# Narrow retention root with VectorE's product from PSUM, and value projections of retention and fox in blocks of 512 columns

## The reference, cut to what matters

```python
q, k, v = h @ w_in[:, rq], h @ w_in[:, rk], h @ w_in[:, rv]      # q and k are rotated, k scaled
o   = causal sum over m of (q_n . k_m) * decay[n, m] * v_m        # the reference does it in chunks of 128
ret = o * rsqrt(mean(o * o, axis=-1) + 1e-6)                      # root mean square of each head
ret_out = silu(h @ w_in[:, rg]) * ret
mix = sigmoid(gate_a) * (nsa_out @ w_proj_a) + sigmoid(gate_b) * (ret_out @ w_proj_b)
```

## Time and profile before

| | |
|---|---|
| median of 3 runs | 2039.71 us (2038.48 to 2040.23) |
| the profiled execution | 2039.96 us |
| its span in the profile | 2037.8 us |
| TensorE busy | 1985.7 us, 97% of the span |
| VectorE, ScalarE, GpSimd busy | 941.1, 730.8, 796.4 us |
| mean granted TensorE clock | 0.99 |

### The profile page before, as it was taken

One profiled execution on the slowest core, in us unless ns is written; L12 is line 12 of the kernel. 1 busy time (PEld: TensorE's weight loads), 2 busy tenths in 40 slices (PEclk: granted clock), 3 DMA queues, 4 the chain that ended last, 5 costly groups with the idle time before them and its releaser, 6 DMA issues.

```text
span 2037.8 us, 25916 instructions
## 1 busy us (share of the span) xinstructions
PE 1985.7 (97%) x9460; PEld 1575.4 (77%) x9460; DVE 941.1 (46%) x1502; ACT 730.8 (36%) x1211; POOL 796.4 (39%) x333
## 2 busy tenths in 40 slices
PE   7999899999999999999999999999999999999998
PEld 6778565688888888888888888776657888888887
DVE  6762655333642464467661105677993341201211
ACT  5233456433431242333313324435544342321321
POOL 4364321144454345435544443231122524444442
PEclk9999999999999999999999999999999999999999
DMA  6355021134757477548633342232122423343341
GB/s 179 83 125 134 21 61 34 36 94 113 185 132 200 119 191 198 142 123 205 174 94 84 102 105 67 67 72 53 32 52 52 104 73 93 93 108 89 93 109 56
DMA packets 156614, 211.16 MB, mean 104 GB/s; under 512 B 15432, under 2 KB 133736, under 8 KB 156392
## 3 DMA queue, kind: packets, MB, share of 16 engines
q1 hardware_dynamic: 142280, 167.34, 33.0%
q10 hardware_dynamic: 14240, 42.54, 7.0%
HBM read 206.69 MB, written 2.10 MB: 102 GB/s over the span
## 4 chain that ended last, share of the span: by engine, by line
PE 48%; issue 31%; POOL 13%; DVE 6%; ACT 1%; DMA 1%; POOLq 0%; ACTq 0%; SPq 0%; DVEq 0%
PE ps L626 15%; PE ps L628 15%; PE ps L627 15%; POOL wlo L590 12%; DVE top L2208 1%; DVE score L2210 1%; DVE ps L2099 1%; PE ps L1044 1%; PE ps L669 1%; PE ps L1067 0%; DMA xrow<-in_x 0%; PE ps L793 0%; PE ps L1087 0%; PE ps L674 0%; DVE score L2193 0%
## 5 line engine op out<-in xcount | busy, mean ns | idle before, releaser
L590 POOL TENSOR_TENSOR wlo<-raw,whi 128x1024 fp32r<-128x1024 f32 (+1 forms) x317 | 781.1, 2479 | 1182.5 <-ACT whi L1336 1160.3
L626 PE MATMUL ps<-hhi,whi 128*128 128x512 f32 x1488 | 590.6, 397 | 5.5 <-DVE hlo L1848 3.3
L628 PE MATMUL ps<-hhi,wlo 128*128 128x512 f32 x1488 | 581.2, 391 | 0.0
L627 PE MATMUL ps<-hlo,whi 128*128 128x512 f32 x1488 | 581.1, 391 | 0.0
L1336 ACT ACTIVATE whi<-raw 128x1024 fp32r<-128x1024 f32 x309 | 316.3, 1054 | 367.9 <-PE ps L628 357.0
L626 PEld LDWEIGHTS ps<-hhi,whi 128*128 128x128 f32 x1488 | 280.7, 189 | 69.8 <-issue 9.3
L628 PEld LDWEIGHTS ps<-hhi,wlo 128*128 128x128 f32 x1488 | 280.4, 188 | 59.4
L627 PEld LDWEIGHTS ps<-hlo,whi 128*128 128x128 f32 x1488 | 280.9, 189 | 57.6 <-issue 1.4
L626 PE MATMUL ps<-hidhi,whi 128*128 (+1 forms) x608 | 236.6, 389 | 0.0
L628 PE MATMUL ps<-hidhi,wlo 128*128 (+1 forms) x608 | 236.5, 389 | 0.0
L627 PE MATMUL ps<-hidlo,whi 128*128 (+1 forms) x608 | 236.5, 389 | 0.0
(11 more groups left out here) (377 smaller groups left out, 2428.6 us busy)
## 6 DMA issues: line engine op xcount, KB each, us to landing
raw<-in_ffn_w SPq DMA_DIRECT2D x264, 256.0 KB, 3.8
raw<-in_w_in SPq DMA_DIRECT2D x154, 256.0 KB, 3.9
trig<-in_ada_w ACTq DMA_DIRECT2D x72, 512.0 KB, 4.5
raw<-in_w_up SPq DMA_DIRECT2D x64, 256.0 KB, 3.9
raw<-in_w_down SPq DMA_DIRECT2D x64, 256.0 KB, 3.9
raw<-in_w_out SPq DMA_DIRECT2D x32, 256.0 KB, 3.9
xrow<-in_x ACTq DMA_DIRECT2D x4, 512.0 KB, 6.8
raw<-in_cmp_k_w SPq DMA_DIRECT2D x8, 256.0 KB, 3.7
```

The source lines that it names most:

```text
L590: last = pool.tensor_tensor(lo, src, hi.bitcast(F32), ALU.subtract)
L626: pe.matmul(out_, lhi, rhi, start=first, stop=False)
L627: pe.matmul(out_, lhi, rlo, start=False, stop=False)
L628: return pe.matmul(out_, llo, rhi, start=False, stop=last)
```

## The change

The mean square of a head becomes a narrow product (four products with one moving column each, into a 128x4 corner of bank 5), so that root and reciprocal work on 128x4; `root_spread` then spreads the reciprocal by four products with the identity into the head's own bank, and VectorE, not GpSimd, multiplies the head by it from PSUM. The steps stand in other places: the roots of heads 0 to 2 and the products of heads 0 and 1 lie in the loop of tiles, head 3 in the attention's round 0, and ScalarE's high parts come one round earlier and more (head 0 ahead of the attention). Both value projections become one block "W" of 512 moving columns with four slabs of 256 rows; the turns of the block before come in its middle.

```diff
-    rvg += [("A", W1["rv"] + 256 * b, 128, ("rv", 256 * b)) for b in range(2)]
+    rvg += [("W", W1["rv"], "rv")]
...
-    dsa += [("A", W2["fv"] + 256 * b, 128, ("fv", 256 * b)) for b in range(2)]
+    dsa += [("W", W2["fv"], "fv")]
...
+                    elif b[0] == "W":
+                        for q in range(4):
+                            load_next(s, w[2 * q * P:2 * (q + 1) * P, b[1]:b[1] + 512].rearrange("(k p) n -> p k n", p=P))
                             s += 1
...
                 for h in range(4):
-                    r, o = SQ[h], rkT[:, h, :]
-                    pool.wait_ge(rt_rcp, h + 1)
-                    pool.tensor_tensor(o, o, r, ALU.mult).then_inc(rt_m, 1)
+                    o = rkT[:, h, :]
                     pool.wait_ge(rt_m, h + 1)
                     pool.wait_ge(pj_silu, h + 1)
                     pool.tensor_tensor(o, o, srg[:, h, :], ALU.mult).then_inc(rt_o, 1)
...
+                        elif b[0] == "W":
+                            banks = []
+                            for q in range(4):
+                                pe.wait_ge(w_split, s + 1)
+                                hi, lo = slab(s, 2)
+                                for t in range(NT):
+                                    if q == 0:
+                                        banks.append(bank(g + t))
+                                    tt = slice(t * P, t * P + P)
+                                    for k in range(2):
+                                        kk = 2 * q + k
+                                        mm = three(ps[:, banks[t], :], hhi[:, kk, tt], hlo[:, kk, tt], hi[:, k, :], lo[:, k, :],
+                                                   kk == 0, kk == 7)
+                                    if q == 3 and t < NT - 1:
+                                        mm.then_inc(pj_mm, 1)
+                                mm.then_inc(w_used, 1)
+                                s += 1
+                                if q == 1:
+                                    post_products(n)
+                            g += NT
+                            continue
...
             def head_sum(h):
                 pe.wait_ge(rt_ev, h + 1)
-                pe.matmul(ps[:, 3 + h % 2, :], cst[:, C_HD128:C_HD128 + P], SQ[h], start=True, stop=True).then_inc(rt_sum, 1)
+                for t in range(NT):
+                    mm = pe.matmul(ps[:, 5, NT * h + t:NT * h + t + 1], SQ[h][:, t * P:t * P + P],
+                                   cst[:, C_HD128:C_HD128 + 1], start=True, stop=True)
+                mm.then_inc(rt_sum, 1)
+
+            def root_spread(h):
+                pe.wait_ge(rt_rcp, h + 1)
+                for t in range(NT):
+                    mm = pe.matmul(ps[:, 3 + h % 2, t * P:t * P + P], root[:, h, t:t + 1].broadcast_to([P, P]), ident,
+                                   start=True, stop=True)
+                mm.then_inc(rt_spread, 1)
...
                     if j == 0 and h >= 2:
-                        pe.wait_ge(rt_root, h - 1)
+                        pe.wait_ge(rt_m, h - 1)
...
                     if x % NT == 2 and 6 <= x:
                         head_sum(x // NT - 1)
+                    if x % NT == 0 and 8 <= x:
+                        root_spread(x // NT - 2)
...
                     if r < n:
                         score_pair(r, 0)
+                        if r == 0:
+                            head_sum(3)
...
                         if part == 1 and r < n:
+                            score_pair(r, 1)
                             if r == 0:
-                                head_sum(3)
-                            score_pair(r, 1)
+                                root_spread(3)
...
+                        if b[0] == "W":
+                            for q in range(2):
+                                high(s + q + SLOTS)
+                            for t in range(NT):
+                                sc.wait_ge(*OUT_DONE[g])
+                                sc.activation(BUF[b[2]][:, t, :], ps[:, g % 4, :], ACT.Copy).then_inc(pj_ev, 1)
+                                g += 1
+                            s += 2
...
                     sc.wait_ge(rt_pv, 4 * h + 4)
+                    sc.activation(SQ[h], ps[:, 3 + h % 2, :], ACT.Square).then_inc(rt_ev, 1)
                     sc.activation(rkT[:, h, :], ps[:, 3 + h % 2, :], ACT.Copy)
-                    sc.activation(SQ[h], ps[:, 3 + h % 2, :], ACT.Square).then_inc(rt_ev, 1)
                     sc.wait_ge(rt_sum, h + 1)
-                    sc.activation(SQ[h], ps[:, 3 + h % 2, :], ACT.Sqrt, bias=col(C_EPS)).then_inc(rt_root, 1)
+                    sc.activation(root[:, h, :], ps[:, 5, NT * h:NT * h + NT], ACT.Sqrt, bias=col(C_EPS)).then_inc(rt_root, 1)
+                retention_high(0)
...
                     if t >= 4:
                         sc.wait_ge(at_pv["nsa"], t - 3)
-                    else:
-                        sc.wait_ge(rt_m, t + 1)
...
-                    for h in {1: (0,), 2: (1,), 3: (2, 3)}.get(r, ()):
+                    for h in {0: (1,), 1: (2,), 2: (3,)}.get(r, ()):
                         retention_high(h)
...
                         x += 1
-                retention_root(0)
+                        if x >= 7 and x % NT == 3:
+                            retention_root(x // NT - 1)
+                        if x >= 9 and x % NT == 1:
+                            retention_scale(x // NT - 2)
+                retention_scale(2)
...
-                ve.reciprocal(SQ[h], SQ[h]).then_inc(rt_rcp, 1)
+                ve.reciprocal(root[:, h, :], root[:, h, :]).then_inc(rt_rcp, 1)
+
+            def retention_scale(h):
+                ve.wait_ge(rt_spread, h + 1)
+                ve.tensor_tensor(rkT[:, h, :], rkT[:, h, :], ps[:, 3 + h % 2, :], ALU.mult).then_inc(rt_m, 1)
...
                         maxima(r, 0)
+                        if r == 0:
+                            retention_root(3)
...
                         maxima(r, 1)
-                        if r < 3:
-                            retention_root(r + 1)
+                        if r == 0:
+                            retention_scale(3)
                         branch_b(r)
```

More of the change, by code:

```diff
@@ L269, in mix_kernel @@
                                                                              "pj_dve", "pj_silu"))
-        rt_qk, rt_sd, rt_pv, rt_ev, rt_sum, rt_root, rt_rcp, rt_m, rt_o, rt_hi, rt_done = (
-            sem(n) for n in ("rt_qk", "rt_sd", "rt_pv", "rt_ev", "rt_sum", "rt_root", "rt_rcp", "rt_m", "rt_o", "rt_hi", "rt_done"))
+        rt_qk, rt_sd, rt_pv, rt_ev, rt_sum, rt_root, rt_rcp, rt_spread, rt_m, rt_o, rt_hi, rt_done = (
+            sem(n) for n in ("rt_qk", "rt_sd", "rt_pv", "rt_ev", "rt_sum", "rt_root", "rt_rcp", "rt_spread", "rt_m", "rt_o", "rt_hi", "rt_done"))
         cm_shift, cm_blk, cm_sig, cm_hid, cm_turn, cm_hidT, cm_out, cm_done = (
@@ L288, in mix_kernel @@
         g = p = r = sl = 0
-        n_out = {"A": 4, "G": 2, "B": 2, "K": 6}
+        n_out = {"A": 4, "G": 2, "B": 2, "K": 6, "W": 4}
         for name, blocks in BL.items():
@@ L327, in mix_kernel @@
             for b in blocks:
-                s += {"A": 2, "B": 2, "K": 1, "G": 0}[b[0]]
+                s += {"A": 2, "B": 2, "K": 1, "G": 0, "W": 4}[b[0]]
                 for x in range(n_out[b[0]]):
-                    if b[0] != "G" and x == {"A": 3, "B": 1, "K": 3}[b[0]]:
+                    if b[0] != "G" and x == {"A": 3, "B": 1, "K": 3, "W": 3}[b[0]]:
                         OUT_DONE[g] = (w_used, s)
@@ L706, in bank, with post_products @@
                     return x % 4
+                def post_products(n):
+                    nonlocal p
+                    for kind, v in turns[n]:
+                        c = chunks[v]
+                        if p >= 4:
+                            pe.wait_ge(pj_dve, p - 3)
+                        if kind == "ms":
+                            pe.wait_ge(pj_ev, out_of[v] + 1)
+                            m = post_ms(name, v)
+                            pe.matmul(ps[:, 4 + p % 4, :], cst[:, C_HD64:C_HD64 + P], SQ[m % 4], start=True, stop=True)\
+                              .then_inc(pj_post, 1)
+                        else:
+                            if c[0] == "rope":
+                                pe.wait_ge(pj_ev, out_of[v] + 1)
+                            else:
+                                pe.wait_ge(pj_dve, post_event[name, "ms", v] + 1)
+                            if name == "nsa" and p == P0["nsa"]:
+                                pe.wait_ge(ld_rest, 16)
+                            perm = c[4] if c[0] == "rope" else c[5]
+                            pe.matmul(ps[:, 4 + p % 4, :], cst[:, perm:perm + P], st[:, v % 4, :], start=True, stop=True)\
+                              .then_inc(pj_post, 1)
+                        p += 1
                 for n in range(len(blocks) + 2):
@@ L785, in projection @@
                                 g += 1
[L786 to L794, removed]
```

(19 more changed lines are left out.)

2 lines of the change are left out of this document (1 added, 1 removed).

## The result

The changed kernel has a median of 2024.12 us over 4 runs (2023.23 to 2024.93), beside 2039.97 us (2038.48 to 2042.08, 4 runs) for the kernel before on the same chip. The ratio is 0.9923, with a 95% interval of 0.9911 to 0.9935: 13 to 18 us faster. The profiled execution took 2024.89 us with a span of 2022.7 us. The forecast was 2024.5.

What follows compares the result with a forecast made beforehand. TensorE, busy 1985.7 of 2037.8 us, was taken as the bound. Terms -3.8 - 3.7 + 2.0 - 9.7 = -15.2 us against the profiled 2039.96 gave 2024.8, forecast as 2024.5, range 2020.5 to 2031.

Steps and rivals of the forecast that it cites:

- Block W for `rv`: At the `rv` projection, 96 wide products in 21.8 us replace two blocks and pauses of 25.5: gain 3.8 us.
- rival B: Skill's price for wide products holds, 0.2 us instead of 1.3 a site: 2.1 us less gain, 2026.6; chance 0.04.
- Block W for `fv`: At the `fv` projection, the block with rotations in its middle ends at 1379.8 for 1383.46: gain 3.7 us.
- the second needs VectorE's norm, done at 1365.2, wait 0 to 0.4: Inside the `fv` block, the second rotation product waits at most 0.4 us for VectorE's 0.75 us norm step.
- W for `fv` from 1346 or so on: Sign expected in the timeline after: the `fv` block starts near 1346, all behind being 12 us earlier.
- The loop: Retention's loop: narrow sums and spreads replace three wide sums on a full TensorE, costing +2.0 us.
- rival C: Coupling in retention's loop: VectorE's product late for heads 2 and 3, sums wait for squares; +3 us, 2027.5; chance 0.12.
- Rounds 0 to 4: Attention's first rounds: without wide reciprocals and GpSimd products, round 5 at 25.6 us instead of 35.75; -9.7 us taken.
- rival A: Attention's start keeps its pauses through the ScalarE-GpSimd chain and stretched normalisations: gain only 9 us, 2030.7; chance 0.13.
- Rival D: Granted clock falls in retention's loop, whose 22.5 us are then worth as much again: slower, 2047; chance 0.03.
- Rival E: Nothing moves in the end, because something late (a load, a slab) sets the pace behind; chance 0.03.
- The range's lower end: 2020.5 us, from retention +1.5, rounds -11, slow stretch behind `fv` shorter by 1.5, and rounding 1.

Runs made afterwards that it cites:

- e1: Kernel before with only the two W blocks, all of retention as before: 2030.87 us, ratio 0.9961.
- e2: Changed kernel with both value projections back in two A blocks, so the retention part alone: 2029.92 us, ratio 0.9949.
- e5: Changed kernel, but ScalarE makes the next slabs' high parts in dsa only after the W block's second slab: 2024.19 us, ratio 0.9913.
- e3: Changed kernel with sums, roots and reciprocals wide again (128x512, no spread) in the new places, VectorE multiplying from SBUF: 2032.15 us, ratio 0.9958.
- e4: Changed kernel with ScalarE's four high parts of retention back in rounds 1, 2, 3 and 3: 2027.3 us, ratio 0.9936.
- e7: Kernel before with eight added products of 512 columns ahead of retention's loop, a pure shift: 2040.04 us, ratio 0.9999.
- e10: The version of e6 run again beside the changed kernel on the same chip: 2022.32 us, ratio to before 0.9912.
- e6: Changed kernel with the held-back slabs of e5 and ScalarE's first high part of retention ahead of its wait for head 3's sum: 2022.48 us, ratio 0.9911.
- e8: Changed kernel with the spreads of heads 0, 1 and 2 done twice: 2026.15 us, ratio 0.9934.

## Why the prediction was right, point by point

**The total** was right, 2024.5 for 2024.12, but not every term, and two errors nearly cancel.

**Block W for `rv`**: 21.76 us, no bank waits, gain 3.8 as forecast. The price of columns was the row's: two blocks of 11.58 less one of 21.76 is 1.4 us, with the same 21.76 in e1 and the same 11.58 in e2. By the Trainium skill, "TensorE: Matmul & The Clock Gate", section "Wait — 56ns, not 53.3ns?", the estimate was 0.2 us a site (rival B). For these forms the traces disagree: 226.7 ns with 512 moving columns and 120.6 with 256.

**Block W for `fv`**: the term that was mis-sized. The step "the second needs VectorE's norm, done at 1365.2, wait 0 to 0.4" took the norm step's length, 0.75 us, from a row in which GpSimd was idle. The norm step ahead of it in the same trace, beside GpSimd's low parts, would have warned:

```profile
1360.03 1.14 DVE L1942 SCALAR_TENSOR_TENSOR st<-st,vec,PT 128x512 f32<-128x512 f32 x1
```

```profile
1358.22 5.21 POOL L590 TENSOR_TENSOR wlo<-raw,whi 128x1024 fp32r<-128x1024 f32 x2 [9.16 <-ACT whi L1336]
```

The change itself lets ScalarE, and behind it GpSimd, start on the next slabs half a block earlier, beside just that step: 1.85 us, a wait of 0.89, and the gain 2.6 instead of 3.7. I had cited such a stretch for the attention and not asked it of `fv`, though the diff moves the two high parts. e5 removes it. The sign "W for `fv` from 1346 or so on" was a slip: 1353.8 less the 11.5 us of the other terms is 1342.3, and W started within 1.5 us of that (1340.75).

**The loop**: +2.3 for +2.0. Sums and spreads did cost 0.81 us for eight records, but the product behind each starts 0.09 us later than behind a wide sum (208.02 to 208.33 for what were 0.22 us). No wait of TensorE in 22.5 us, also for heads 2 and 3: rival C has nothing. The margin is as thin as I had called it: VectorE's product with head 0 ends at 212.05 and head 2's first value product starts at 212.46, 0.4 us later, where I had counted 0.3.

**Rounds 0 to 4**: -9.3 for -9.7, and by the mechanism named: three long reciprocals out of the rounds and the fourth short (e3), high parts one round apart (e4). How the 9.3 divide between the reciprocals and GpSimd's four products is open. Round 0 went as worked out: sum of head 3 after a wait of 0.35, first exponential and second score pair at 4.38 us behind the first (forecast 4.2), round 1 at 7.2 (6.8), round 2 at 11.2 (10.6), round 5 at 26.4 (25.6). The normalisations beside GpSimd never held TensorE over 0.33 us, so rival A did not come; e4 is that rival made true, by placing two high parts in one round, and it cost 2.8 us in the rounds and 3 in time.

**Rival D** (clock in the loop): granted clock 1.00 in both stretches. **Rival E**: the gain arrived whole at the end.

**What I did not see**: that untouched stretches differ by 2 us and more between two executions. I subtracted from one profiled execution, which from round 5 to the second norm is slower than all eleven other traces, also than that of its own program shifted (e7). The terms -3.7 and -9.7 were too large by 1.5 together, the loop's too small by 0.3, and those 1.9 us filled the hole. That the total came within 0.4 us was luck; the parts alone would have given 2026.3, still in the range. The range's lower end was 0.3 us too high by its own sum: 0.5 + 1.3 + 1.5 + 1 below 2024.5 is 2020.2.

## What to carry to other kernels

When a step that stands in every partition's row (a root, a reciprocal of a sum) is broadcast before it is computed, compute it narrow and broadcast by TensorE afterwards: here 3.34 us of VectorE became 0.18 (and 0.69 for the product that it took over from GpSimd), for 0.9 us on TensorE. It paid because TensorE was waiting for ScalarE, VectorE and GpSimd elsewhere and the chain could be hidden behind tiles. When work is moved, price every engine's step at the new place with what now runs beside it, above all two-tensor steps of VectorE beside GpSimd. And when parts are summed from traces, compare the untouched stretches before believing the remainder, between the same two products and not between the same two times; a granted clock that differs is not yet a difference in time (0.91 for 1.00 cost 0.1 us at most at a norm here).

## What the runs showed of the hardware that I had not expected

The same pause of 2.48 us in the same code kept the granted clock at 1.00 over the next 6 us in one execution and went with 0.72 in another (before, e7). At the second norm, over the same part of the program, the granted clock is 0.83 in two traces (before, e5), 0.91 in eight (e1 to e4, e7 to e10) and 1.00 in two (after, e6); TensorE is busy for all of the 20 us at 0.83 and 0.91 (19.9 of them in e10) and for 19 at 1.00, where it waits for VectorE. The changed kernel itself has 1.00 in one trace and 0.91 in the other. The runs of one kernel spread over 1.7 to 10.4 us; of the 13 runs of before beside e5 to e8 the shortest (span 2033.8 us) has a mean granted clock of 0.993 and the longest (2041.6) one of 0.989.

Narrow groups of plain f32 products cost a little more than their own eight records. Behind the sum's one-column products the value product starts 0.31 us after the score product ahead of it (208.02 to 208.33), where it is 0.22 behind a wide sum. In e8 each doubled spread lengthens the loop by 0.89 us, where eight such records elsewhere step by 0.81.

VectorE's product of 128x512 with two inputs from SBUF took 2.65 to 2.71 us beside GpSimd's low parts and 0.69 with GpSimd idle; with one input from PSUM it took 0.69 beside them too (e5).
